# Expert gathers of two slots for 64 tokens, and their products in pairs on the two column halves of TensorE

## The chip, the cores and the metric

The kernel runs on one core of a Trainium2 chip. The metric is the device time of one execution in microseconds (us), the median of several runs. Engines are called as in the profile: PE (TensorE, matrix products; PEld its weight loads), DVE (VectorE), ACT (ScalarE), POOL (GpSimd, which here issues the gathers), SP (SyncE, which issues the weight loads), and 16 DMA engines.

## What is computed

A diffusion backbone of two layers on 256 context tokens and 256 latent tokens, D = 1024, all in float32. Each layer is a modulated norm, attention (two head groups), an output projection, and then an expert feed-forward (PEER). The second layer leaves out the context's outputs. The change is in the expert part, for which six blocks of 128 tokens are worked through (four in layer 0, two in layer 1):

```python
q = (xb @ p['peer_wq']).reshape(PEER_CHUNK, PEER_HEADS, 2, PEER_KEY_HALF)
s = jnp.einsum('thcd,ckd->thck', q, p['peer_subkeys'])
sv, si = lax.top_k(s, PEER_TOPK)
...
top_s, pos = lax.top_k(cand_s, PEER_TOPK)
eidx = ...                                   # 8 heads x 16 = 128 experts per token
gate = jax.nn.softmax(top_s, axis=-1)
u = jnp.take(p['peer_u'], eidx, axis=0)
v = jnp.take(p['peer_v'], eidx, axis=0)
act = jax.nn.gelu(jnp.einsum('ted,td->te', u, xb), approximate=False) * gate
return jnp.einsum('te,ted->td', act, v)
```

So each token takes 128 rows of 8 KB (u and v side by side) out of a table, and the whole kernel gathers 768 times 128 rows.

## The kernel before

**Slots.** A block has 128 slots. Slot i of a block is the i-th expert of each of its 128 tokens, one token per partition. POOL (unit, L613) copies eight slots' indices from IDX to FIX (L626) and issues one indirect DMA per slot (L634) into one of the eight buffers of the ring EXPERT; before it, it waits until the buffer's last user is done. DVE (dot, L1541) multiplies the u half of the buffer with H2, the block's normed tokens, and sums: one dot product per token. ACT (weigh, L1117) takes the GELU (L1122), multiplies with the gate (L1124), and for three slots of four scales the identity by the result to DIAG (L1129, three buffers). PE (apply, L932) multiplies DIAG with the v half into the two banks VSUM (L937), which sums the slots. Every fourth slot's product is DVE's instead (apply, L1548, line L1554), added to ACC after the next slot's dot product. After 128 slots `close` (L1576) adds both sums, multiplies with the modulation's gate, which PE broadcasts from a diagonal matrix GD (L813), and adds to the tokens X. The next block's first slots stand behind it on DVE, and its first product on PE waits until both banks are read.

**Picks.** For each head and tile, `top` (L1479) finds the 16 best experts on DVE, ACT's `gate_exps` (L1112) takes their exponentials with the sum (TE, TSUM), and `experts` (L1513) turns positions into expert indices: two small operations and a conversion (L1518), six wide ones on one-hot tables (L1174, L1527), the inverse of the sum (L1529), and then GATE (L1535) and IDX (L1537). DVE waits for ACT's sum just ahead of L1529. On ACT the exponential stands behind the weighing of the slots ahead of it and needs another table than GELU.

**Weights.** SP loads weights in pieces of up to 512 KB into the five buffers of WT (WSLOTS), each as soon as PE has released the piece five before it. Where the projections use them: L797, L825, and L927 for the picks' queries (two pieces per head).

**The order of the work.** A plan written out by code, one list of stages, is walked by all engines. `weave` (L189) spreads slots evenly through the background (picks, projections, attention of the next tiles) by a table of costs. ACT and DVE follow `late(PLAN)`, in which slots stand earlier by up to three (LEAD_SLOTS) than on PE. Stages of the plan: front (norm and input projections), attention (L850, L1062, L1366), outward (output projection, norm, and `back`, which turns the normed tokens for H2, L1247), pick. Gathers run from 244 us to the end, except while the modulation products of layer 1 (`ada`, L740: matmuls on four groups of 32 columns, L755) use the ring's buffers, 1840 to 1990 us. In time: picks at 244 to 345 us, attention to 410, output projection to 480, picks to 590, the latents' front to 775, attention to 915, output to 1025, picks to 1370, layer 1's front to 1835; after the modulation picks to 2125, front and attention to 2280, output to 2345, and picks to the end.

A float32 product is two instructions in the trace: a slot's two products of 128x512 are four MATMULs.

## Time and profile before

| | |
|---|---|
| median of 3 runs | 2744.06 us (2742.5 to 2751.88) |
| the profiled execution | 2754.68 us, its span 2752.7 us |
| PE busy | 2116.2 us, 77% of the span, clock 0.892 |
| DVE busy | 1852.3 us, 67% |
| ACT busy | 1146.0 us, 42% |
| POOL busy | 973.3 us, 35% |
| DMA | 976.17 MB, mean 355 GB/s; 855.69 MB of it by POOL's queue |
| chain that ended last | PE 31%, DVE 24%, DMA 23%, ACT 13% |

A profile is one execution. The busy share of an engine is a mean over stretches with different limits. The chain is followed back from the last instruction, at each step to what released it. The clock is the part of full speed that was granted to PE. A DMA share is that of the 16 engines' time; it can come out a little above 1.

### The profile page before, as it was taken

How to read it: one execution, taken by the hardware profiler on the slowest of the kernel's cores; microseconds unless marked ns; L12 is line 12 of the kernel's file. 1: busy time of each engine (PE TensorE's matmuls, PEld its weight loads, DVE VectorE, ACT ScalarE, POOL GpSimd, SP SyncE). 2: the span in 40 equal slices, each digit the busy share in tenths (PEclk: the TensorE clock that was granted, in tenths of full speed). 3: DMA queues.
4: the chain of work that ended last, by engine and by line, in shares of the span. 5: the costliest groups of instructions: out<-in, count | busy, mean ns of one | idle time of the engine just before them, and what ended most of it. 6: DMA issues, size and time to landing. Idle time of an engine off the chain costs nothing.

```text
span 2752.7 us, 26089 instructions
## 1 busy us (share of the span) xinstructions
PE 2116.2 (77%) x6768; PEld 1091.3 (40%) x6768; DVE 1852.3 (67%) x4482; ACT 1146.0 (42%) x3024; POOL 973.3 (35%) x916
## 2 busy tenths in 40 slices
PE   6997788779898987777677777768777887767765
PEld 2455434534444444343233332334544444433321
DVE  0145985975678769888956565543389696877775
ACT  2122483452388444344452342322135573433432
POOL 1012343333344333344443443420033443444443
PEclk8988889889999999889899999988788999888989
DMA  8467989989899899899998999994299999999997
GB/s 323 136 235 304 387 338 357 389 320 383 318 380 343 326 369 375 355 418 416 415 420 363 418 394 414 413 386 155 75 355 400 393 369 396 402 392 420 421 416 296
DMA packets 210712, 976.17 MB, mean 355 GB/s; under 512 B 17532, under 2 KB 70296, under 8 KB 112280
## 3 DMA queue, kind: packets, MB, share of 16 engines
q0 software_dynamic: 123648, 855.69, 77.2%
q1 hardware_dynamic: 86936, 118.99, 12.6%
q8 instruction: 54, 0.88, 0.1%
q14 instruction: 74, 0.61, 0.1%
HBM read 973.56 MB, written 1.05 MB: 354 GB/s over the span
## 4 chain that ended last, share of the span: by engine, by line
PE 31%; DVE 24%; DMA 23%; ACT 13%; issue 7%; POOL 1%; POOLq 0%; SPq 0%; DVEq 0%; ACTq 0%
DMA EXPERT<-in_peer_uv,FIX 21%; PE VS L937 11%; PE PA L797 9%; DVE EXPERT L1544 8%; DVE ACC L1554 3%; PE PA L825 2%; DVE SCR L1174 2%; ACT L1122 2%; PE PB L927 2%; DMA EXPERT<-in_w_ada 2%; ACT L1070 1%; ACT WEI L1124 1%; ACT HT L1026 1%; ACT DIAG L1129 1%; PE VS L755 1%
## 5 line engine op out<-in xcount | busy, mean ns | idle before, releaser
L937 PE MATMUL VS<-EXPERT,DIAG 128*128 128x512 f32 x2304 | 1185.8, 656 | 322.3 <-ACT DIAG L1129 322.1
L634 POOL DMA_INDIRECT EXPERT<-in_peer_uv,FIX x768 | 899.4, 1171 | 1169.7 <-PE VS L937 760.3
L1544 DVE CUSTOM_DVE_ANT_0 EXPERT<-EXPERT,H 128x1024 f32<-128x1024 f32 x768 | 925.5, 1223 | 363.3 <-DMA EXPERT<-in_peer_uv,FIX 354.4
L937 PEld LDWEIGHTS VS<-EXPERT,DIAG 128*128 128x128 f32 x2304 | 457.1, 209 | 920.2 <-issue 468.2
L1122 ACT ACTIVATE GEL<-DOT 128x1 f32<-128x1 f32 x768 | 155.3, 202 | 1060.3 <-DVE DOT L1544 1059.5
L797 PE MATMUL PA<-WT,HT 128*128 128x512 f32 (+2 forms) x768 | 328.0, 574 | 31.2 <-ACT KTD L1052 10.4
L1554 DVE SCALAR_TENSOR_TENSOR ACC<-EXPERT,WEI,ACC 128x1024 f32<-128x1024 f32 x192 | 246.0, 1281 | 40.6 <-ACT WEI L1124 39.9
L1129 ACT ACTIVATE DIAG<-IDN,WEI 128x128 f32<-128x128 f32 x576 | 231.3, 402 | 74.0 <-PE VS L937 56.0
L1124 ACT ACTIVATE WEI<-GEL,GATE 128x1 f32<-128x1 f32 x768 | 226.3, 295 | 25.0
L797 PEld LDWEIGHTS PA<-WT,HT 128*128 128x128 f32 x768 | 150.7, 199 | 193.8 <-issue 140.2
L927 PE MATMUL PB<-HT,WT 128*128 128x128 f32 (+1 forms) x1280 | 204.3, 320 | 10.4 <-issue 10.4
L927 PEld LDWEIGHTS PB<-HT,WT 128*128 128x128 f32 x1280 | 192.4, 216 | 36.6 <-issue 30.0
L626 POOL COPY FIX<-IDX 128x8 uint32 (+1 forms) x96 | 39.1, 408 | 316.1 <-PE VS L937 179.9
L1122 ACT ACT_TABLE_LOAD x115 | 147.5, 1283 | 6.6 <-ACT SCR L1070 0.8
L664 POOL DMA_DIRECT2D EXPERT<-in_w_ada x48 | 34.6, 722 | 262.3 <-PE VS L755 193.8
L726 PE MATMUL PB<-IDN,SCR 128*128 128x128 f32 (+1 forms) x374 | 58.8, 305 | 74.7 <-ACT SCR L1015 21.9
L726 PEld LDWEIGHTS PB<-IDN,SCR 128*128 128x128 f32 (+1 forms) x374 | 47.5, 152 | 107.4 <-ACT SCR L1015 28.0
L908 PE MATMUL PA<-SKT,SCR 128*128 128x128 f32 x192 | 37.9, 338 | 59.1 <-ACT SCR L1106 59.1
L1070 ACT ACTIVATE SCR<-PB,NM 128x512 f32<-128x512 f32 (+1 forms) x96 | 58.8, 614 | 52.7 <-DVE NM L1392 52.0
L825 PE MATMUL PA<-WT,HT 128*128 128x512 f32 (+1 forms) x136 | 67.2, 645 | 16.3 <-ACT HT L1058 8.7
L755 PE MATMUL VS<-EXPERT 128*32 128x512 f32 x384 | 55.5, 688 | 22.1 <-DMA EXPERT<-in_w_ada 22.1
L1375 DVE TENSOR_REDUCE MX<-PB 128x1 f32<-128x512 f32 (+1 forms) x96 | 55.4, 596 | 22.2 <-PE PB L865 22.0
(140 smaller groups left out, 1715.6 us busy)
## 6 DMA issues: line engine op xcount, KB each, us to landing
EXPERT<-in_w_ada POOLq DMA_DIRECT2D x48, 1024.0 KB, 10.2
WT<-in_peer_wq SPq DMA_DIRECT2D x80, 512.0 KB, 15.4
WT<-in_w_in SPq DMA_DIRECT2D x56, 512.0 KB, 10.9
WT<-in_w_out SPq DMA_DIRECT2D x40, 512.0 KB, 7.7
EXPERT<-in_peer_uv,FIX POOLq DMA_INDIRECT x768, 11.6
WT<-in_w_in SPq DMA_DIRECT2D x16, 384.0 KB, 9.7
WT<-in_w_in SPq DMA_DIRECT2D x20, 288.0 KB, 6.9
WT<-in_mla_wk_up SPq DMA_DIRECT2D x5, 512.0 KB, 10.2
```

The costliest lines, as they stand in the source:

```text
L634: pool.indirect_dma_start(out=EXPERT[:, j, :], out_offset=None, in_=a["peer_uv"], in_offset=bass.IndirectOffsetOnAxis(ap=FIX[:, par, j:j + ...
L726: last = nc.tensor.transpose(bank[0:rows, i * P:(i + 1) * P], s, IDN[:, :])
L797: last = nc.tensor.matmul(bank[:, 0:n], HT[:, k, t * P:(t + 1) * P], w[:, k % KP, 0:n], start=(k == 0), stop=(k == KD - 1))
L825: last = nc.tensor.matmul(bank[:, 0:n], HT[:, k0 + k, t * P:(t + 1) * P], w[:, k % KP, 0:n], start=(k == 0), stop=(k == kn - 1))
L927: last = nc.tensor.matmul(bank[:, mine], held["w"][k // HP][:, k % HP, c * P:(c + 1) * P], HT[:, k, mine], start=(k == 0), stop=(k == KD - 1))
L937: ins = nc.tensor.matmul(VSUM[n][:, :], DIAG[:, i, :], EXPERT[:, j, D + n * W:D + (n + 1) * W], start=first, stop=last_one)
L1070: ins = nc.scalar.activation(PR[:, h % 2, c, 0:keys], bank[:, 0:keys], ACT.Exp, bias=NM[:, h % 2, c:c + 1], scale=SC_M if h < MH else SC_D ...
L1122: nc.scalar.activation(GEL[:, one], DOT[:, j:j + 1], ACT.Gelu).then_inc(gelu_ready, 1)
L1124: nc.scalar.activation(WEI[:, one], GEL[:, one], ACT.Copy, scale=gate).then_inc(wei_ready, 1)
L1129: nc.scalar.activation(DIAG[:, i, :], IDN[:, :], ACT.Copy, scale=WEI[:, one]).then_inc(diag_ready, 1)
L1544: nc.vector.tensor_tensor_reduce(out=EXPERT[:, j, 0:D], in0=EXPERT[:, j, 0:D], in1=H2[:, b % HB, :], scale=1.0, scalar=0.0, op0=ALU.mult, ...
L1554: nc.vector.scalar_tensor_tensor(out=ACC[:, :], in0=EXPERT[:, j, D:2 * D], scalar=WEI[:, BY_PE:BY_PE + 1], in1=ACC[:, :], op0=ALU.mult, op ...
```

## The change

A gather now brings two slots for 64 tokens. Partitions 0 to 63 hold the even slot and 64 to 127 the odd slot of the same 64 tokens; of two gathers that follow each other the first (g = 0) is for tokens 0 to 63, the second for 64 to 127. Sizes and number of the gathers stay. For this IDX and GATE are written in four pieces each (64 partitions, every second column), GATE by ACT, which waits for DVE's inverse, now taken right behind the conversion L1518. H2 holds each half of the tokens twice (four copies in place of one) and has two blocks instead of three, so the last `back` of layer 0 moves behind the picks. DIAG is 128x64, one for each of the ring's eight buffers, scaled from TWO, two stacked identities. PE takes two gathers at a time, with matmuls that write partitions 0 to 63 and 64 to 127 of VSUM in turn. All products are PE's; ACC shrinks to 512 columns and serves `close` alone. WT has four buffers instead of five, and LEAD_SLOTS is four.

```diff
-WSLOTS = 5
+WSLOTS = 4
...
-HB = 3
+HB = 2
+IB = 3
+G = P // 2
...
-LEAD_SLOTS = 3
+LEAD_SLOTS = 4
...
-            def apply(no, i, j, first=False, last_one=False):
-                pe.wait_ge(diag_ready, no + 1)
+            def apply(no, j, first=False, last_one=False):
+                pe.wait_ge(diag_ready, no + 2)
                 for n in range(2):
-                    ins = nc.tensor.matmul(VSUM[n][:, :], DIAG[:, i, :], EXPERT[:, j, D + n * W:D + (n + 1) * W],
-                                           start=first, stop=last_one)
-                ins.then_inc(used_pe, 1)
+                    for g in range(2):
+                        ins = nc.tensor.matmul(VSUM[n][g * G:(g + 1) * G, :], DIAG[:, j + g, :],
+                                               EXPERT[:, j + g, D + n * W:D + (n + 1) * W], start=first, stop=last_one)
+                        if n == 1:
+                            ins.then_inc(used_pe, 1)
...
+                act.wait_ge(inverse_ready, tick("inverse"))
+                for g2 in range(2):
+                    mine = slice(g2 * G, (g2 + 1) * G)
+                    parted = TE[mine, t, :].rearrange("p (q s) -> p q s", s=2)
+                    for s in range(2):
+                        to = GATE[s * G:(s + 1) * G, b % IB, h * TOPK:(h + 1) * TOPK].rearrange("p (q g) -> p q g", g=2)
+                        ins = nc.scalar.activation(to[:, :, g2], parted[:, :, s], ACT.Copy, scale=TINV[mine, t:t + 1])
+                link(ins)
...
-                if i < BY_PE:
-                    act.wait_ge(wei_ready, no + 1)
-                    if not isinstance(mine, int) or mine >= BY_PE:
-                        act.wait_ge(used_pe, mine - BY_PE + 1)
-                    nc.scalar.activation(DIAG[:, i, :], IDN[:, :], ACT.Copy, scale=WEI[:, one]).then_inc(diag_ready, 1)
+                act.wait_ge(wei_ready, no + 1)
+                nc.scalar.activation(DIAG[:, j, :], TWO[:, :], ACT.Copy, scale=WEI[:, one]).then_inc(diag_ready, 1)
...
-                    nc.vector.tensor_copy(H2[:, b % HB, half * W:(half + 1) * W], bank[:, :]).then_inc(emptied_a, 1)
+                    for g2 in range(2):
+                        for s in range(2):
+                            ins = nc.vector.tensor_copy(H2[s * G:(s + 1) * G, b % HB, g2, half * W:(half + 1) * W],
+                                                        bank[g2 * G:(g2 + 1) * G, :])
+                    ins.then_inc(emptied_a, 1)
...
                 after(mark(nc.vector.tensor_copy(ABF[:, :, :], AB[:, :, :])))
+                dve.wait_ge(topexp_ready, tick("topexp"))
+                nc.vector.reciprocal(TINV[:, t:t + 1], TSUM[:, t:t + 1]).then_inc(inverse_ready, 1)
...
-                dve.wait_ge(topexp_ready, tick("topexp"))
-                inverted = mark(nc.vector.reciprocal(TINV[:, t:t + 1], TSUM[:, t:t + 1]))
                 after(found)
-                at = slice(h * TOPK, (h + 1) * TOPK)
...
-                after(inverted)
-                nc.vector.tensor_scalar(GATE[:, b % HB, at], TE[:, t, :], TINV[:, t:t + 1], None, ALU.mult)
                 after(both)
-                nc.vector.tensor_scalar(IDX[:, b % HB, at], PICK[:, 0, :], float(l * NK * NK), None, ALU.add)\
-                    .then_inc(idx_ready[t], 1)
+                for g2 in range(2):
+                    parted = PICK[g2 * G:(g2 + 1) * G, 0, :].rearrange("p (q s) -> p q s", s=2)
+                    for s in range(2):
+                        to = IDX[s * G:(s + 1) * G, b % IB, h * TOPK:(h + 1) * TOPK].rearrange("p (q g) -> p q g", g=2)
+                        ins = nc.vector.tensor_scalar(to[:, :, g2], parted[:, :, s], float(l * NK * NK), None, ALU.add)
+                ins.then_inc(idx_ready[t], 1)
...
                 diagonals(l, tile // 2, 2, 0)
-                dve.wait_ge(used_dve, (b + 1) * QUADS)
-                dve.wait_ge(used_pe, (b + 1) * QUADS * BY_PE)
                 for n in range(2):
                     half = slice(n * W, (n + 1) * W)
-                    if n == 1:
-                        diagonals(l, tile // 2, 2, n)
-                    tt(ACC[:, half], ACC[:, half], VSUM[n][:, :], ALU.add).then_inc(vsum_read, 1)
                     rows = from_a()
+                    link(nc.vector.tensor_copy(ACC[:, :], rows[:, :]))
+                    free_a()
+                    if n == 0:
+                        diagonals(l, tile // 2, 2, 1)
+                        dve.wait_ge(used_pe, (b + 1) * SLOTS)
+                    tt(ACC[:, :], VSUM[n][:, :], ACC[:, :], ALU.mult).then_inc(vsum_read, 1)
                     dve.wait_ge(vsum_read, 2 * b + n + 1)
-                    link(tt(ACC[:, half], ACC[:, half], rows[:, :], ALU.mult))
-                    free_a()
                     x = X[:, tile, half]
-                    ins = tt(x, x, ACC[:, half], ALU.add)
+                    ins = tt(x, x, ACC[:, :], ALU.add)
```

## Rows read from the trace of the kernel before

**Rows 1.** Table by stretch: stretch, us, busy PE, PEld, DVE, ACT, POOL; clock, DMA share, GB/s.
```profile
345.00:410.00 65.00, 52.41 (x165) 25.71 (x164) 52.39 (x131) 57.34 (x117) 26.57 (x22) 0.89 0.89 334
410.00:480.00 70.00, 57.12 (x189) 30.94 (x188) 42.03 (x88) 28.11 (x77) 23.50 (x24) 0.93 0.95 357
480.00:590.00 110.00, 79.62 (x333) 52.63 (x331) 104.61 (x365) 54.85 (x133) 38.85 (x36) 0.86 0.98 381
590.00:700.00 110.00, 99.89 (x244) 45.75 (x244) 54.36 (x88) 35.25 (x109) 34.55 (x33) 0.95 0.92 352
700.00:775.00 75.00, 61.31 (x196) 33.97 (x197) 53.37 (x101) 31.23 (x90) 25.24 (x24) 0.91 0.82 327
775.00:915.00 140.00, 122.21 (x470) 65.42 (x469) 117.75 (x245) 121.36 (x230) 54.41 (x48) 0.98 0.89 339
915.00:1025.00 110.00, 96.82 (x295) 50.97 (x294) 72.32 (x129) 47.91 (x134) 42.20 (x40) 0.95 0.95 363
1025.00:1110.00 85.00, 66.99 (x188) 36.18 (x187) 83.33 (x281) 41.05 (x104) 32.17 (x32) 0.90 0.97 380
1110.00:1835.00 725.00, 533.00 (x1254) 242.26 (x1253) 497.97 (x1055) 274.69 (x822) 308.89 (x287) 0.88 0.99 402
...
2040.00:2125.00 85.00, 61.09 (x228) 37.44 (x226) 80.18 (x271) 42.18 (x110) 32.40 (x32) 0.86 1.02 412
2125.00:2345.00 220.00, 179.35 (x580) 93.33 (x581) 156.62 (x298) 122.32 (x299) 84.92 (x77) 0.92 0.96 383
2345.00:2740.00 395.00, 272.02 (x713) 120.69 (x711) 290.94 (x639) 147.62 (x455) 184.35 (x164) 0.89 0.98 403
```

**Rows 2.** Chain of waits by line, 605 to 700 us and 775 to 915 us.
```profile
by line: PE PA L797 55.4%; PE VS L937 36.1%; DVE SCR L1174 2.2%; DVE SCR L1298 1.2%; ACT QTD L1052 1.1%; ACT KTD L1052 1.1%; PE PB L726 0.9%; issue 0.9%; DVE SCR L1307 0.5%; ACT HT L1026 0.4%; DVEq L1317 0.1%; DVE SS L1307 0.1%; DVEq L1170 
...
by line: ACT L1122 12.8%; ACT L1070 11.9%; DVE EXPERT L1544 11.4%; ACT SCR L1070 8.3%; issue 7.0%; DVE ACC L1554 5.3%; PE VS L937 5.2%; DVE MX L1375 5.2%; PE PB L865 4.6%; DVE SCR L1389 4.4%; ACT WEI L1124 3.7%; PE PA L873 3.5%; ACT GEL L11
```

**Rows 3.** Expert product in the chain; PE around the modulation product: start, us, line, count.
```profile
647.36 1.72 PE VS L937 x4
...
1994.03 3.74 PE L927 MATMUL PB<-HT,WT 128*128 128x128 f32 x32
1997.70 3.64 PE L755 MATMUL VS<-EXPERT 128*32 128x512 f32 x32
```

**Rows 4.** Groups by form: line, engine, operation, count; busy us, mean ns; idle before.
```profile
L1554 DVE SCALAR_TENSOR_TENSOR ACC<-EXPERT,WEI,ACC 128x1024 f32<-128x1024 f32 x192 | 246.0, 1281 | 40.6 <-ACT WEI L1124 39.9 <-DVE SCR L1293 0.3 <-DVE EXPERT L1210 0.2
...
L1129 ACT ACTIVATE DIAG<-IDN,WEI 128x128 f32<-128x128 f32 x576 | 231.3, 402 | 74.0 <-PE VS L937 56.0
L1124 ACT ACTIVATE WEI<-GEL,GATE 128x1 f32<-128x1 f32 x768 | 226.3, 295 | 25.0
```

**Rows 5.** One pick in order of time, DVE and ACT: start, us, engine, line.
```profile
2072.08 0.18 DVE L1518 CAST ABF<-AB 128x32 f32<-128x32 uint32 x1
...
2073.97 0.19 ACT L1114 ACTIVATION_READ_ACCUMULATOR TE<-TS,NT 128x1 f32 x1
...
2074.30 0.15 DVE L1529 RECIPROCAL TINV<-TSUM 128x1 f32<-128x1 f32 x1
...
2075.00 1.23 DVE L1544 CUSTOM_DVE_ANT_0 EXPERT<-EXPERT,H 128x1024 f32<-128x1024 f32 x1
```

**Rows 6.** Closing block 0 on DVE, in order of time, to the next block's first slot.
```profile
700.68 1.28 DVE L1554 SCALAR_TENSOR_TENSOR ACC<-EXPERT,WEI,ACC 128x1024 f32<-128x1024 f32 x1
...
708.12 0.69 DVE L1174 TENSOR_TENSOR ACC<-ACC,PA 128x512 f32<-128x512 f32 x1 [1.57 <-PE PA L813]
...
710.88 1.22 DVE L1544 CUSTOM_DVE_ANT_0 EXPERT<-EXPERT,H 128x1024 f32<-128x1024 f32 x1
```

**Rows 7.** Group by form: the copies to H2.
```profile
L1252 DVE COPY H<-PA 128x512 f32<-128x512 f32 x12 | 7.9, 687 | 19.8 <-PE PA L726 19.7
```

**Rows 8.** A weight piece in the chain, and PE's wait for it in order of time.
```profile
2142.66 16.42 DMA WT<-in_w_in
...
2159.12 1.56 PE L797 MATMUL PA<-WT,HT 128*128 128x384 f32 x4 [1.75 <-DMA WT<-in_w_in]
```

92 lines of the change are left out of this document (38 added, 54 removed).

## The prediction

> **What bounds the kernel now.** I read three views in order. First the table by stretch [rows 1], which splits the time in which experts are gathered. The reader should compare, line by line, the share of the DMA engines with the busy times of DVE, PE and ACT: where the DMA share is close to 1 the gathers themselves set the pace, and nothing that an engine saves there is worth anything. That holds for 1110 to 1835 us and 2345 to 2740 us, 1120 us together (0.99 and 0.98 with the closes in them). In the rest the share is 0.82 to 0.98, and an order of work that is interleaved with the gathers sets the pace. Second, the chain of waits of two such stretches [rows 2]: 605 to 700 us is PE alone (input projection 55.4%, expert products 36.1%); 775 to 915 us is attention, where ACT leads (two table loads per head and slot, L1070 and L1122, 24.7%) and DVE's share of the expert product (L1554) has 5.3%. Third, the picks (480 to 590, 1025 to 1110, 2040 to 2125 us in [rows 1]): DVE is busy 104.61 of 110, 83.33 of 85 and 80.18 of 85 us. There DVE sets the pace, with DMA close behind (0.97 to 1.02).
>
> If every stretch of [rows 1] with a share below 1.01 came up to it (its length times the part that it lacks), 345 to 410 gives 7.7 us, 410 to 480 4.2, 480 to 590 3.3, 590 to 700 9.8, 700 to 775 14.1, 775 to 915 16.6, 915 to 1025 6.5, 1025 to 1110 3.4, 1110 to 1835 14.4, 2125 to 2345 10.9 and 2345 to 2740 11.7: about 103 us. That is the ceiling of any gain here.
>
> **The products on PE.** A slot's product is now four matmul instructions of 128x512 in 1.72 us at full clock [rows 3], for three slots in four: 1.29 us per slot on average. Afterwards two slots are eight instructions on 64 columns each. If the two column halves run side by side they take about 1.72 us for two slots, 0.86 us per slot; if not, 3.44 us, 1.72 per slot. The nearest row is the modulation product L755 on four column groups of 32: 32 instructions in 3.64 us, 0.11 us each [rows 3], a quarter of the 0.43 us of a full-width one. So column groups do overlap in this kernel with the same operand shapes, and I take 0.86, a saving of 0.43 us per slot, and keep 1.72 as the other end. A switch of form seems free: L755 starts at 1997.70 us, 0.07 us before the modelled end of the work ahead of it (1994.03 + 3.74) [rows 3]. The Trainium skill, page "TensorEngine Tiling (Array Packing)", section "Key Properties", speaks against this: changing the tiling mode drains the engine. It has no price; here there would be two switches per pair, 768 in all, and the row shows none that can be read.
>
> Where PE leads and DMA has room are 410 to 480, 590 to 700 and 915 to 1025 us, by the plan some 17 + 30 + 30 slots. The saving is 77 x 0.43 / 0.94 (clock) = 35 us on PE, but DMA room there is 4.2 + 9.8 + 6.5 = 20.5 us, and some of the time in them is spent waiting for norms and gates, not PE. I take 12 us (ends 4 and 20).
>
> **DVE without its quarter.** 192 products of 1.281 us [rows 4] leave DVE, 1.20 us each from start to start. In attention (345 to 410, 775 to 915, about half of 2125 to 2345) they stand on the chain with about 5% [rows 2], as does PE's product (5.2%), while ACT is busy 57 of 65 and 121 of 140 us and gets more: DIAG for four slots in four instead of three, at half the width. At 0.402 us for 128 columns and 0.295 us for one [rows 4] 64 columns come to about 0.35 us: 4 x 0.35 against 3 x 0.40 is +0.05 us per slot, 5 us for the 96 slots. Out of 320 us, 5% is 16 us for the DVE share and 5 us for PE's third, minus 5 for ACT, with room on DMA of 7.7 + 16.6 + 5: I take 13 us saved (ends 3 and 25).
>
> **The handshake in each pick.** This speaks against the change. Before, DVE reads ACT's exp sum only after its six wide operations on the one-hot tables; GATE is then DVE's. Afterwards DVE waits for the sum right behind the conversion L1518, inverts it for ACT, and does the wide operations after that. In [rows 5] the conversion ends at 2072.26, ACT's sum at 2074.16 us. ACT can't be earlier: it has just weighed the slot whose dot product DVE did before the pick, and then loads a table. That gap was covered by DVE's own 2.04 us (2072.26 to 2074.30); now it is bare. The same rows can be read for 48 picks, and 43 have such a gap, of 1.1 to 2.3 us; where it is short of 2.3 the last slot had no DIAG, which it now gets (0.35 us). Behind the inverse come 2.04 us of wide operations, 0.1 and four small IDX writes of 0.1 each where one stood. From 2072.26 to the next dot product at 2075.00 is 2.74 us now; afterwards 1.90 + 0.35 + 0.15 + 2.04 + 0.1 + 0.5 = 5.0. That is +2.3 here, between +1.6 and +2.4 in the others, 2.1 on average. Queued behind the wait on DVE are the next dot products, so ACT, PE and POOL wait for it too. ACT's four GATE pieces (under 0.3 us each by WEI [rows 4]) lie beside the wide operations and cost nothing; without that cover 1.2 us per pick.
> In the picks that DVE paces (25, between 275 and 345, 480 and 590, 1025 and 1110, 2040 and 2125 us) that is +53 us, against 26 DVE products less, 26 x 1.20 = 31 us: **+21 us** (ends +8, if ring and DMA took part of it, and +30). In the others (1110 to 1370, 2345 to 2740) DMA leads and DVE has the time: 4.7 slots or more save 1.4 and the pick costs 2.1, while DVE is busy 69 and 74% of those two stretches [rows 1]: nothing.
>
> **Closing a block.** A close takes DVE from 700.68 to 710.88 us [rows 6], 10.2 us with the ring full and POOL idle. It loses the product (1.2) and the memset ahead of the first slot, and the second gate diagonal is made before the first half is finished, so that PE's second broadcast no longer waits for it (1.57 us of idle DVE [rows 6]): 7 to 8 us are left. Against that the first pair of the next block needs two dot products before PE starts. For blocks 0 to 3 I take 2.3 us each, 9 us. For blocks 4 and 5, closed right behind their last slot, PE's last pair (1.7 us after ACT's DIAG) is now on the way to the broadcast, and eats the gain: 0.
>
> **Copies for H2.** One copy of 0.687 us [rows 7] becomes four on 64 partitions, of the same free size: 8 instead of 2 per block, +3.7 us on DVE, six times. DVE is idle a third of the time or more around them (410 to 480, 915 to 1025 us, the prologue) and one is put behind the picks: 2 us in all, 22 if nothing hid them.
>
> **Four weight buffers for five.** Pieces of w_in take up to 16.42 us on the chain [rows 8], and PE already waited 1.75 us with five buffers. Issue to use shrinks by one piece. At 12 pieces between 2133 and 2175 us, each limited to latency over buffers, 16.4/4 - 16.4/5 = 0.8 us, 10 us; elsewhere pieces are further apart (3.4 us and more) or come sooner. The output projection at 2280 adds a little. I take 8 us (ends 0 and 18). Moving slots one further ahead of the background in late() (LEAD_SLOTS 4) is to pay for the pair's delay; I count both as 0 (ends -5 and +5), since a slot that waits for the next product was already there, one in four.
>
> **Sum.** -12 - 13 + 21 - 9 + 2 + 8 = **-3 us** against the span of 2752.7 us (2754.68 us for that execution), so about 2750 us there. The profiled execution lies 10.6 us above the median of the runs, 2744.06; the same sum from the median gives **2741 us**.
>
> **Rivals.**
> A, relief to the DMA limit: with two engines relieved at once, everything outside the picks comes up close to DMA's pace. Of the ceiling of 103 us, 96 lie outside the picks; two thirds of it, 62 us, less 21 for the picks and 8 for weights is -33: 2711 us. For it: in 775 to 915 us all three engines are busy 84 to 87%, so chains between them, not one engine, hold it up. Against it: ACT's table loads stay.
> B, slower: the bare wait for the exp sum. It decides as soon as it exceeds what a cycle of picks loses, 1.2 us per pick with four slots. With the long end for the picks (+30), the weights at +15, and relief of only 25 us in all: +20, 2764 us. For it: DVE at 94 to 98% in those stretches [rows 1].
> C, the change doesn't do what it says: the halves don't overlap, 0.43 us more per slot instead of less. 77 slots cost 35 us instead of gaining 12, attention about 10 more: some 60 us above, 2800 us. Against it stands L755 [rows 3].
> D, the clock: granted 0.98 in 775 to 915 us, where PE is busy 87%, and 0.86 to 0.90 in the picks with 72 to 79% [rows 1]. With PE at 75% in attention it may fall to that level, and take 10% of PE's work back, about 5 us; it is inside the range of the forecast. The Trainium skill, "TensorE: Matmul & The Clock Gate", section "What's actually happening", says that activity releases a throttle, of two levels; by that rule this loss comes too, and the trace agrees in its direction.
>
> **How the numbers follow.** Forecast with its spread (2727 to 2757) 0.42, A 0.30, B 0.21, C 0.07. A change of under 0.3%, 8 us (2736 to 2752), is what a measurement of this kernel can't tell from none. Of the forecast's own case about a quarter lies below, over half inside, a fifth above. Faster: 0.30 + 0.10 = 0.40. Slower: 0.21 + 0.07 + 0.08 = 0.36. Same: 0.24. The range from 2700 to 2777 leaves out C and the far ends of A and B; the forecast's own is 2727 to 2757.
>
> **What the changed profile would show.** The product line on PE: 128x64 instructions, eight in about 1.9 us, and PE's busy time down (overlap counted once); 3.4 us per pair would prove C. DVE's reciprocal L1529 with 80 to 90 us idle before it, released by ACT's TE, against 5 now: if it is under 30, the pick step is wrong and the kernel faster by up to 20 us. Pick cycles 1 us longer. Attention and projections with a DMA share up by some hundredths: if not, relief was worth nothing. PE waits for WT in 2130 to 2170 us longer than 1.75 us. The DMA-paced stretches with the same time per gather: if they are slower, holding two slots at a time drained the ring, which I count at nothing.

## The result, and the profile after

The change makes the kernel slower: 2850.48 us, median of the runs (2848.94 to 2861.48), against 2743.72 us (2742.5 to 2751.88) for the kernel before on the same chip. The ratio is 1.0386, with a 95% interval from 1.0359 to 1.0413: 106 us. The forecast was 2741 us with a range from 2700 to 2777. The profiled execution took 2851.5 us, its span is 2849.7 us.

Head of the profile of the kernel after:

```profile
span 2849.7 us, 27355 instructions
...
PE 1941.4 (68%) x7536; PEld 878.7 (31%) x7536; DVE 1670.7 (59%) x4417; ACT 1241.4 (44%) x3408; POOL 926.7 (33%) x916
...
PE 30%; DMA 25%; DVE 21%; ACT 16%; issue 6%; POOL 2%; POOLq 0%; SPq 0%; DVEq 0%; ACTq 0%; PEld 0%
```

PE has 175 us less to do than before (2116.2) and DVE 182 us less (1852.3); ACT has 95 us more (1146.0 before), at 44% of the span. The kernel takes 97 us more by the two spans. So the loss isn't work of PE or DVE; those two wait. The table by stretch says where. The columns are those of [rows 1]; the stretches are cut so that they hold about the same slots as lines there (by DVE's dot products to within 4, for example 38 against 41 in attention and 27 against 31 in the picks of 480 to 590 us):

```profile
359.00:431.00 72.00, 49.76 (x188) 21.15 (x188) 47.71 (x126) 61.66 (x132) 24.42 (x24) 0.80 0.80 298
431.00:500.00 69.00, 52.98 (x218) 25.44 (x220) 38.92 (x84) 25.80 (x77) 20.36 (x22) 0.85 0.95 365
500.00:615.00 115.00, 70.18 (x338) 44.14 (x334) 93.35 (x364) 58.07 (x157) 34.15 (x33) 0.81 0.89 343
...
812.00:945.00 133.00, 111.97 (x478) 54.65 (x478) 97.84 (x215) 115.12 (x225) 45.77 (x43) 0.86 0.79 307
945.00:1060.00 115.00, 90.70 (x319) 43.25 (x316) 64.86 (x124) 50.46 (x146) 42.80 (x40) 0.88 0.92 357
1060.00:1155.00 95.00, 63.67 (x230) 28.03 (x228) 78.04 (x284) 48.03 (x134) 36.29 (x34) 0.79 0.90 354
1155.00:1875.00 720.00, 445.96 (x1474) 160.59 (x1473) 423.98 (x1006) 292.78 (x910) 293.12 (x281) 0.82 0.96 391
2078.00:2184.00 106.00, 64.44 (x288) 36.31 (x284) 83.14 (x304) 51.08 (x146) 35.49 (x34) 0.76 0.93 365
2184.00:2420.00 236.00, 173.86 (x675) 76.08 (x671) 140.54 (x288) 129.69 (x323) 85.83 (x83) 0.86 0.92 364
```

Read the DMA share (the last but one number) against [rows 1]. It was to rise wherever engines held it down; it rose nowhere, stayed at 0.95 in the output projection (410 to 480) and fell in the other eight lines: picks of 480 to 590 us from 0.98 to 0.89 and of 1025 to 1110 from 0.97 to 0.90, attention of 775 to 915 from 0.89 to 0.79, and even the DMA-paced 1110 to 1835 from 0.99 to 0.96. In the picks DVE is now busy 93.35 of 115 us, no longer 104.61 of 110: it doesn't set the pace by its work any more, it waits.

The delay can also be counted by slots, as the start of the same slot's dot product on DVE in the two traces. By the times of before it is 11.2 us at 345, 13.0 at 480, 28.8 at 590, still 28.7 at 915, 36.0 at 1025, 46.9 at slot 256 (1118 us), 52.7 at slot 512 (2014 us), 81.0 at 2345 and 95.2 at the last slot. So the picks of 480 to 590 us lose 16 us and those of 1025 to 1110 lose 11, the stretch from 2014 to 2345 us 28, attention at 775 to 915 nothing, and the two DMA-paced stretches 6 and 14.

The groups of the change, by form (as [rows 4]): busy time, mean ns, idle time just before:

```profile
L936 PE MATMUL VS<-EXPERT,DIAG 128*64 128x512 f32 x3072 | 917.2, 733 | 464.3 <-ACT DIAG L1137 456.1
L1137 ACT ACTIVATE DIAG<-TWO,WEI 128x64 f32<-128x64 f32 x768 | 267.0, 348 | 25.0
L1125 ACT ACTIVATE GATE<-TE,TINV 64x8 f32<-64x8 f32 x192 | 57.5, 300 | 18.8 <-DVE TINV L1532 15.7 <-issue 1.3
L1550 DVE TENSOR_SCALAR IDX<-PICK 64x8 uint32<-64x8 f32 x192 | 33.5, 174 | 3.5
L1262 DVE COPY H<-PA 64x512 f32<-64x512 f32 x48 | 33.1, 689 | 22.5 <-PE PA L724 21.8
...
L1532 DVE RECIPROCAL TINV<-TSUM 128x1 f32<-128x1 f32 x48 | 7.9, 164 | 100.9 <-ACT TE L1117 93.5 <-issue 7.1
```

The durations are as forecast: DIAG 348 ns (0.35 was taken), the H2 copy 689 ns as [rows 7], an IDX piece 174 ns (0.1 was taken). The inverse has 100.9 us of idle time before it, 2.1 per pick, 93.5 of it put down to ACT's exp sum. And the two waits that grew, from the list of waits (total us, times, longest), of before and then of after:

```profile
POOL EXPERT L634 <- PE VS L937: 760.3, 300, 15.4
DVE EXPERT L1544 <- DMA EXPERT<-in_peer_uv,FIX: 354.4, 270, 4.5
POOL EXPERT L634 <- DVE ACC L1554: 194.6, 76, 7.6
POOL FIX L626 <- PE VS L937: 179.9, 60, 15.6
```

```profile
POOL EXPERT L634 <- PE VS L936: 928.1, 214, 17.6
DVE EXPERT L1557 <- DMA EXPERT<-in_peer_uv,FIX: 550.6, 362, 7.7
...
POOL FIX L629 <- PE VS L936: 323.0, 75, 21.5
```

POOL waits for a free buffer 116 us longer (928.1 + 323.0 against 760.3 + 194.6 + 179.9), and DVE waits 196 us longer for a gather to land. PE has less to do and releases buffers later. That is the shape of the loss: the ring is held by something that isn't PE's or DVE's work.

Do the halves overlap at all? One pair in the output of the timeline, in order of time:

```profile
660.20 1.94 PE L936 MATMUL VS<-EXPERT,DIAG 128*64 128x512 f32 x8
...
662.07 2.41 PE L795 MATMUL PA<-WT,HT 128*128 128x512 f32 x5
```

Eight instructions in 1.87 us from start to start, where one full-width slot took 1.72 us for four [rows 3], both with the full clock granted. They do.

### The profile page after: what moved, and what is told of

Its sections match the earlier page's. It is cut to its first block, busy times and chain, and to the rows that moved or that the text cites. A ratio compares the mean times of both kernels' runs of the same rounds, so it can differ in the third digit from the quotient of the medians.

```text
span 2849.7 us, 27355 instructions
## 1 busy us (share of the span) xinstructions
PE 1941.4 (68%) x7536; PEld 878.7 (31%) x7536; DVE 1670.7 (59%) x4417; ACT 1241.4 (44%) x3408; POOL 926.7 (33%) x916
## 4 chain that ended last, share of the span: by engine, by line
PE 30%; DMA 25%; DVE 21%; ACT 16%; issue 6%; POOL 2%; POOLq 0%; SPq 0%; DVEq 0%; ACTq 0%; PEld 0%
DMA EXPERT<-in_peer_uv,FIX 23%; PE VS L936 11%; PE PA L795 9%; DVE EXPERT L1557 8%; DVE SCR L1181 3%; ACT L1133 2%; PE PA L823 2%; ACT WEI L1135 2%; ACT L1071 2%; ACT DIAG L1137 2%; ACT L1117 2%; ACT HT L1027 1%; POOL EXPERT L634 1%; PE PB L925 1%; DMA EXPERT<-in_w_ada 1%
## 5 line engine op out<-in xcount | busy, mean ns | idle before, releaser
L634 POOL DMA_INDIRECT EXPERT<-in_peer_uv,FIX x768 | 860.5, 1120 | 1173.4 <-PE VS L936 928.1
L936 PE MATMUL VS<-EXPERT,DIAG 128*64 128x512 f32 x3072 | 917.2, 733 | 464.3 <-ACT DIAG L1137 456.1
L936 PEld LDWEIGHTS VS<-EXPERT,DIAG 128*64 128x64 f32 x3072 | 226.2, 162 | 1024.0 <-ACT DIAG L1137 606.1
L795 PE MATMUL PA<-WT,HT 128*128 128x512 f32 (+2 forms) x768 | 347.0, 601 | 44.5 <-ACT KTD L1053 20.3
L1137 ACT ACTIVATE DIAG<-TWO,WEI 128x64 f32<-128x64 f32 x768 | 267.0, 348 | 25.0
L925 PE MATMUL PB<-HT,WT 128*128 128x128 f32 (+1 forms) x1280 | 219.0, 335 | 25.6 <-issue 20.8
L925 PEld LDWEIGHTS PB<-HT,WT 128*128 128x128 f32 x1280 | 199.5, 226 | 64.0 <-issue 49.1
L629 POOL COPY FIX<-IDX 128x8 uint32 (+1 forms) x96 | 31.4, 327 | 451.9 <-PE VS L936 323.0
L724 PEld LDWEIGHTS PB<-IDN,SCR 128*128 128x128 f32 (+1 forms) x374 | 50.2, 162 | 148.7 <-ACT SCR L1016 46.9
L823 PE MATMUL PA<-WT,HT 128*128 128x512 f32 (+1 forms) x136 | 67.7, 649 | 22.4 <-ACT QTM L1048 11.2
L906 PEld LDWEIGHTS PA<-SKT,SCR 128*128 128x128 f32 x192 | 33.3, 251 | 141.3 <-ACT SCR L1107 126.9
```

What stands on the lines that cost most here:

```text
L634: pool.indirect_dma_start(out=EXPERT[:, j, :], out_offset=None, in_=a["peer_uv"], in_offset=bass.IndirectOffsetOnAxis(ap=FIX[:, par, j:j + ...
L724: last = nc.tensor.transpose(bank[0:rows, i * P:(i + 1) * P], s, IDN[:, :])
L795: last = nc.tensor.matmul(bank[:, 0:n], HT[:, k, t * P:(t + 1) * P], w[:, k % KP, 0:n], start=(k == 0), stop=(k == KD - 1))
L823: last = nc.tensor.matmul(bank[:, 0:n], HT[:, k0 + k, t * P:(t + 1) * P], w[:, k % KP, 0:n], start=(k == 0), stop=(k == kn - 1))
L925: last = nc.tensor.matmul(bank[:, mine], held["w"][k // HP][:, k % HP, c * P:(c + 1) * P], HT[:, k, mine], start=(k == 0), stop=(k == KD - 1))
L936: ins = nc.tensor.matmul(VSUM[n][g * G:(g + 1) * G, :], DIAG[:, j + g, :], EXPERT[:, j + g, D + n * W:D + (n + 1) * W], start=first, stop= ...
```

## The experiments

All runs come with their own runs of the kernel before (median 2745.1 to 2747.2 us by batch). Differences below are made from the ratios, times 2745 us. By the intervals of the two ratios a difference between two runs is uncertain by some 10 to 15 us to either side, and by 6 to 9 where both have ten executions. Line names are those of the kernel that is edited.

### The three parts of the change, each undone

**Inverse late, GATE on DVE.** In the changed kernel, the order of before in a pick, with GATE in four pieces on DVE:

```diff
-                dve.wait_ge(topexp_ready, tick("topexp"))
-                nc.vector.reciprocal(TINV[:, t:t + 1], TSUM[:, t:t + 1]).then_inc(inverse_ready, 1)
...
+                dve.wait_ge(topexp_ready, tick("topexp"))
+                inverted = mark(nc.vector.reciprocal(TINV[:, t:t + 1], TSUM[:, t:t + 1]))
```

> The kernel after, but DVE takes the inverse after the wide operations again and writes GATE itself in four pieces; ACT no longer waits for the inverse. Theory handshake (the bare wait for the exp sum on DVE makes most of the loss): idle of DVE ahead of the reciprocal falls from 101 us to under 10, and the time from 2850 to 2800 us or less. Theory pair (a slot that waits for its partner keeps its buffer, the ring of eight runs dry): 2835 us or more, since the ring is not touched. Theory weights (four buffers): no more than 10 us.

Measured: 2818.88 us (2817.03 to 2821.65), ratio 1.0262 [1.0233, 1.0291]. 34 us of the 106 come back, between the two numbers (2800 for the wait as most of the loss, 2835 for the pair). DVE's idle time ahead of the inverse falls from 100.9 to 13.5 us. GATE moves from ACT to DVE in the same edit, so the 34 us are those of both.

**Single slots.** PE takes each slot as soon as its DIAG is ready; halves, ring and order stay:

```diff
-                pe.wait_ge(diag_ready, no + 2)
+                pe.wait_ge(diag_ready, no + 1)
+                g = j % 2
...
-                            for k in range(0, TOPK, 2):
+                            for k in range(TOPK):
```

> The kernel after, but PE takes each slot as soon as its DIAG is ready, two products on one column half, instead of waiting for two slots. A lone slot costs PE 1.72 us at full clock instead of 0.86. Theory pair: buffers come free earlier, 2850 falls to 2810 us or less in spite of PE's dearer products. Theory handshake: 2840 to 2860 us, as PE is not the bound of the picks. If PE time were the bound: slower than 2860 us.

Measured: 2817.61 us (2815.06 to 2821.0), ratio 1.0258 [1.0229, 1.0288]: 35 us, as much as the item before, and I had counted it at 0. The theory of the pair wanted 2810 us or less, that of the wait 2840 or more; it lies nearer to the first. PE's products take 1155.4 us instead of 917.2, that is 238 us more work on PE, and the kernel is faster. One place shows why, first in the kernel after (DVE's dot of the first slot of a pair, the dot of the second behind the pick, the product):

```profile
1385.68 1.23 DVE L1557 CUSTOM_DVE_ANT_0 EXPERT<-EXPERT,H 128x1024 f32<-128x1024 f32 x1 [1.78 <-DMA EXPERT<-in_peer_uv,FIX]
...
1389.67 0.16 DVE L1532 RECIPROCAL TINV<-TSUM 128x1 f32<-128x1 f32 x1 [2.38 <-ACT TE L1117]
...
1392.80 1.22 DVE L1557 CUSTOM_DVE_ANT_0 EXPERT<-EXPERT,H 128x1024 f32<-128x1024 f32 x1
...
1396.37 5.90 PE L936 MATMUL VS<-EXPERT,DIAG 128*64 128x512 f32 x14 [9.55 <-ACT DIAG L1137]
```

and the same slot with single products:

```profile
1383.00 1.23 DVE L1556 CUSTOM_DVE_ANT_0 EXPERT<-EXPERT,H 128x1024 f32<-128x1024 f32 x1 [1.26 <-DMA EXPERT<-in_peer_uv,FIX]
...
1385.23 1.93 PE L936 MATMUL VS<-EXPERT,DIAG 128*64 128x512 f32 x4 [0.56 <-ACT DIAG L1136]
```

From dot to product it is 10.7 us in the first and 2.2 in the second. The order by single slots puts the second half of a pick between the two slots of a pair; the first one's buffer is held through it. Counted over DVE's whole timeline, 20 of the 48 inverses stand behind an odd number of dots, that is inside a pair.

**Both undone.** 

> The kernel after with both edits tried alone: inverse and GATE late and on DVE, and each slot's product as soon as its DIAG is ready. If handshake and pair cost each their own (32 and 33 us alone) the two add up: 2785 us. If both show one and the same wait: 2815 us.

Measured: 2791.05 us (2789.31 to 2806.23), ratio 1.0173 [1.0138, 1.0209]: 58 us of 106. The parts nearly add up (69 by themselves), nearer to the 2785 us of two separate costs than to 2815.

**Five weight buffers in the changed kernel.** DIAG is laid into the used-up u half of the ring buffer, which makes room for the fifth:

```diff
-WSLOTS = 4
+WSLOTS = 5
-        DIAG = sb("DIAG", [P, RING, G])
+        DIAG = EXPERT[:, :, 0:G]
```

> The kernel after with five weight buffers. The room comes from DIAG, which lies in the spent u half of its ring buffer instead of a tile of its own; instructions and waits are the same. Theory weights, by the 45 us that four buffers cost the kernel before: 2850 falls to 2805 to 2815 us, first in the picks of block 0 and in the slots 27 to 50 of block 4. Theory handshake or pair alone: 2840 us or more, as the prefetch then hides behind other waits.

Measured: 2838.72 us (2834.51 to 2854.68), ratio 1.0341 [1.03, 1.0382]: 12 us, no more than the uncertainty of such a difference. With the two edits above as well:

> The changed kernel with late inverse and GATE on DVE, each slot's product as soon as its DIAG is ready, and five weight buffers instead of four. The same without the fifth buffer ran at 2791 us; the kernel before at 2744 to 2747 us. Theory 1 (the weight buffers cost the changed kernel as much as the kernel before, 42 us, once the pair and the early wait no longer hide it): 2750 to 2760 us, and the change is explained but for some 10 us. Theory 2 (in the changed kernel the fifth buffer is worth 12 us only, as it was with the pairs): 2779 us, and some 32 us stay for the copies to H2, the four pieces of IDX and GATE, the order with four slots ahead.

Measured: 2769.94 us (2764.96 to 2777.34), ratio 1.0088 [1.0058, 1.0119]. Here the fifth buffer is worth 23 us: neither of the two numbers, but nearer to the small one. With the 47 us below, the order is that it pays more the less else holds the kernel up; the step from 12 to 23 alone isn't clear of noise.

### The same parts, put into the kernel before

**The early wait alone.** The wait and L1529 of the kernel before moved behind L1518, nothing else:

> The kernel before, with nothing changed but the place of the wait for the exp sum and of the reciprocal on DVE: right behind the conversion, as in the kernel after. GATE stays on DVE. Theory handshake as forecast: 26 picks that DVE paces lose about 2 us each, 2744 to 2795 us; by the long end 85 us. Theory pair or weights: the wait is taken up by the ring, under 2760 us.

Measured: 2802.35 us (2789.76 to 2805.3), ratio 1.0184 [1.0144, 1.0225]: 51 us, between 40 and 62 by the interval. The gross price of the forecast was 53. DVE's idle time before the inverse goes from 5.2 to 89.6 us.

**Four weight buffers alone** (`WSLOTS = 4`):

> The kernel before with four weight buffers instead of five, nothing else. Forecast was 8 us, ends 0 and 18: 2744 to 2752 us. Theory weights (the smaller prefetch makes most of the loss): 2790 us or more.

Measured: 2788.64 us (2784.11 to 2806.67), ratio 1.0171 [1.0121, 1.0221]: 47 us, where the forecast had 8. The groups that changed are those of the picks' queries, the kernel before first, then the run with one place of its timeline:

```profile
L927 PE MATMUL PB<-HT,WT 128*128 128x128 f32 (+1 forms) x1280 | 204.3, 320 | 10.4 <-issue 10.4
L1106 ACT COPY SCR<-PB 128x128 f32<-128x128 f32 (+1 forms) x80 | 21.9, 273 | 67.3 <-PE PB L927 67.1
```

```profile
L927 PE MATMUL PB<-HT,WT 128*128 128x128 f32 (+1 forms) x1280 | 201.2, 317 | 58.3 <-issue 58.3
L1106 ACT COPY SCR<-PB 128x128 f32<-128x128 f32 (+1 forms) x80 | 22.0, 275 | 118.2 <-PE PB L927 118.2
...
503.80 3.75 PE L927 MATMUL PB<-HT,WT 128*128 128x128 f32 x16 [9.02 <-issue]
507.59 0.27 ACT L1106 COPY SCR<-PB 128x128 f32<-128x128 f32 x1 [10.59 <-PE PB L927]
...
510.12 0.94 POOL L634 DMA_INDIRECT EXPERT<-in_peer_uv,FIX  x1 [18.55 <-PE VS L937]
```

PE's idle time before the query product goes from 10.4 to 58.3 us, and only the number of weight buffers differs. The trace files it under "issue"; that it is the landing of these pieces is concluded from the edit, as the trace doesn't name them. Each head wants two pieces of 512 KB, and a piece takes 15.4 us to land (median of the page's DMA issues of before), while a piece is issued only when the one four before it is released. While PE stands there, ACT stands behind it in L1106 with the weighing of the next slots queued behind (the 10.59 us above), and POOL behind these (18.55 us without a free buffer).

**Six weight buffers.** In the kernel before, with H2 in two blocks to make room:

> The kernel before with six weight buffers instead of five, paid for by H2 with two blocks instead of three, for which the last turn of the latents' tokens goes behind the picks, as in the change. Theory 1 (weight loads between gathers are limited by their latency over the number of buffers, and five is short too): part of the 42 us that the fifth buffer brought comes again, 2715 to 2735 us, faster than the kernel before. Theory 2 (five covers the latency, and the step from four to five is where it ended): 2740 to 2750 us, or some us more for the moved turn.

Measured: 2745.66 us (2738.3 to 2759.28), ratio 1.0007 [0.9984, 1.0029]. No gain, as the second theory had it: five is deep enough here, and the moved `back`, which is part of this edit, costs nothing that shows.

**All products on PE.** The kernel before with the fourth slot's product on PE too, at full width, by single slots:

> The kernel before with DVE's quarter of the products on PE at full width, one slot at a time: no pairs, no new layout, five weight buffers, the late wait. DVE loses 192 x 1.2 us, PE gains 192 x 1.72 us. By the forecast's terms the picks gain 31 us, the closes 6, attention 10, the stretches that PE paces lose 20: 2715 to 2730 us. If relief of DVE is worth nothing: 2745 us or more.

Measured: 2757.96 us (2748.25 to 2765.63), ratio 1.0033 [1.0016, 1.0051]: 9 us slower. By slot it is 8.4 us ahead at slot 97 of block 0 (its dot starts at 578.6 us against 587.0), behind the picks, and loses that and more in the front and the attention that follow (7.9 us behind at slot 200). Taking the products off DVE and putting them on PE brings nothing.

**The same with DIAG in the ring**, eight instead of four:

> Single slots at full width, all on PE, as in the run of 2758 us, with DIAG in the ring (eight). ACT waited 135 us for PE before a DIAG there. Theory 1 (these waits are slack that comes back as a later wait of PE): 2752 to 2762 us. Theory 2 (they held up the weighing and the exponentials of the picks behind them on ACT): 2735 to 2748 us, as fast as the kernel before or a little faster.

Measured: 2753.84 us (2744.39 to 2769.05), ratio 1.0044 [1.0017, 1.007]; not to be told from the run before it. At slot 97 it is 9.7 us ahead of the kernel before, 5.3 behind at slot 200.

### What the pair costs

**Pairs at full width.** The run above with four DIAG buffers, PE taking two slots at a time:

```diff
-                pe.wait_ge(diag_ready, no + 1)
+                pe.wait_ge(diag_ready, no + 2)
```

> The kernel before with all products on PE at full width, five weight buffers and the late wait, as in the run that came to 2758 us, but PE takes two slots at a time, as in the change, behind the second one's DIAG. Nothing of the halves, of the four-piece writes or of the copies. Theory 1 (holding the first slot of a pair is the cost, 33 us in the changed kernel): 2780 to 2800 us. Theory 2 (the 33 us belonged to the column halves, for example to the drain between forms or to the weights of 64 columns): no difference, 2755 to 2762 us.

Measured: 2850.38 us (2846.02 to 2852.67), ratio 1.0369 [1.0336, 1.0401]: 92 us more than with single slots, far outside both numbers. That run had a flaw: a pair of DIAGs held two of four buffers, and ACT waited 269.9 us for PE ahead of a DIAG, against 135.2. So with DIAG in the ring:

> Products in pairs at full width, all on PE, as in the run of 2850 us, but DIAG is written into the ring buffer's used-up u half, so there are eight and ACT never waits for PE before a DIAG. Theory 1 (most of the 92 us that pairing cost at full width was the lack of DIAG buffers, and holding a slot costs about what it costs in the changed kernel): 2785 to 2800 us. Theory 2 (a pair of full-width products, 3.4 us on PE in one piece, is itself the cost, and the halves are what makes pairs bearable): 2830 us or more.

Measured: 2824.12 us (2819.34 to 2835.88), ratio 1.0286 [1.0241, 1.033]: 66 us more than single slots with the same DIAGs. That lies between the two numbers: lack of DIAG explains 23 us of the 92 (8 to 38 by the intervals), the pair itself the rest. At full width the second slot costs PE another 1.72 us in one piece. On the halves a pair costs 35 us, 24 with the inverse late (2818.88 against 2791.05), although single slots take that gain in PE's time away; the halves don't turn the pair into a gain. How much of the step from 66 to 35 is due to them isn't shown, as the two kernels differ in more.

**Slots placed in pairs.** The plan and `late` put slots two at a time, so no pick comes between them:

```diff
-    return [("slots", b, i, i + 1) for i in range(first, last)] + ([("close", b)] if last == SLOTS else [])
+    return [("slots", b, i, i + 2) for i in range(first, last, 2)] + ([("close", b)] if last == SLOTS else [])
```

> The changed kernel with the order by single slots replaced by one by pairs: the plan and the earlier order of ACT and DVE hold slots two at a time, so both slots of a pair stand next to each other on every engine. Everything else stays. The changed kernel stands at 2850 us. Theory 1 (what the pair costs is that its first slot is held in the ring until the second, which the interleaved order puts a background step later): placing them side by side gives most of the 33 us back that taking single slots gave, so 2815 to 2830 us. Theory 2 (what the pair costs is the release of two ring buffers at a time and a product that starts two dot products late, wherever the slots stand): 2845 us or more, and up to 2870 us, since the background steps between slots then come in larger lumps.

Measured: 2835.83 us (2829.74 to 2838.68), ratio 1.0312 [1.028, 1.0345]: 20 us back, between the theories. With late inverse and five weight buffers:

> The changed kernel with late inverse and GATE on DVE, five weight buffers, and the order by pairs; products stay in pairs on the two column halves. If the order by pairs undoes the hold of the first slot, it comes to the time of the same kernel with single slots, 2750 to 2780 us. If the pair itself costs, some 30 us more, 2790 to 2810 us.

Measured: 2792.52 us (2785.88 to 2794.96), ratio 1.0156 [1.0123, 1.019]: 19 us above the same kernel with single slots in the order by slots (2769.94), as the second theory had it. With the lead of four slots a pair costs even side by side.

### The lead of the slots

**Three ahead instead of four**, with late inverse, single slots, five buffers (`LEAD_SLOTS = 3`):

> The changed kernel with late inverse, single slots and five weight buffers (2770 us), with slots three ahead on ACT and DVE instead of four. Theory 1 (the order with four ahead puts dots in front of work that is due, and holds the rest of the gap to the kernel before): 2755 to 2762 us. Theory 2 (the rest is the four-piece copies and index writes and the products that PE takes over): 2767 to 2777 us.

Measured: 2760.48 us (2752.2 to 2771.48), ratio 1.0054 [1.0033, 1.0075]: 9 us. **One pair ahead instead of two**, with the order by pairs (`LEAD_SLOTS = 2`):

> Pairs on the two halves, order by pairs, late inverse, five weight buffers (2792 us), with one pair of slots ahead on ACT and DVE in place of two. Theory 1 (the lead is too long, as with single slots, where three in place of four gave 9 us): 2775 to 2785 us. Theory 2 (a pair needs the lead, since PE waits for its second slot): 2795 us or more. To beat the kernel before it would have to come under 2740 us, which neither expects.

Measured: 2751.21 us (2747.19 to 2757.36), ratio 1.0021 [1.0008, 1.0034]: 37 us from one number in the order, more than either theory had. The two traces part most between slots 384 and 512, by 29 of 35 us, and one place in layer 1's front shows how. First with four ahead (PE's transpose, then the products behind it, POOL, and ACT's copy, for which PE waits):

```profile
1626.71 1.53 ACT L1048 COPY KTM<-PB 96x512 f32<-96x512 f32 x3
...
1627.33 1.09 PE L724 MATMUL PB<-IDN,SCR 128*96 128x128 f32 x4 [13.36 <-ACT KTM L1048]
1628.35 9.32 PE L936 MATMUL VS<-EXPERT 128*64 128x512 f32 x32
...
1632.83 0.94 POOL L634 DMA_INDIRECT EXPERT<-in_peer_uv,FIX  x1 [16.11 <-PE VS L936]
```

and with two ahead, for the same transpose:

```profile
1607.96 1.53 ACT L1048 COPY KTM<-PB 96x512 f32<-96x512 f32 x3
...
1608.58 1.09 PE L724 MATMUL PB<-IDN,SCR 128*96 128x128 f32 x4 [6.26 <-ACT KTM L1048]
...
1614.09 0.94 POOL L634 DMA_INDIRECT EXPERT<-in_peer_uv,FIX  x1 [9.91 <-PE VS L936]
```

Each slot that is placed ahead of this copy on ACT brings a wait for its gather, one per 2.49 us here. Six such weighings stand ahead of it in the first trace from 1612.70 us on, PE can't go on to the products of these very slots before its transpose, and all eight buffers are held until it does: POOL issues nothing for 16 us.

**And single slots on top:**

> The same with PE taking each slot as soon as its DIAG is ready. With the order by single slots and three ahead this kernel ran at 2760 us. Theory 1 (what the pair costs, even side by side, is that two ring buffers come free late and together): 10 to 20 us under the run beside it. Theory 2 (placed side by side, a pair costs nothing more and only the halves' overlap counts): the same as the run beside it or up to 10 us above it.

Measured: 2741.88 us (2733.05 to 2746.39), ratio 0.998 [0.9962, 0.9997]: 11 us under the run with pairs. It is the only variant of the change whose time isn't above that of the kernel before. It is ahead by 5 us, less than the 0.3% that a measurement of this kernel can tell from nothing.

### The clock

The granted clock went from 0.892 to 0.825 with the change. Behind each pair two products of full width with zero weights were added, which change nothing in the sum, to keep PE busy:

```diff
+                if not last_one:
+                    for n in range(2):
+                        nc.tensor.matmul(VSUM[n][:, :], ZERO[:, :], SKT[:, :, :].rearrange("p i n -> p (i n)"),
+                                         start=False, stop=False)
```

> The kernel after with two further full-width products of 128x512 behind each pair, with zeros as weights, so that PE has as much to do as with single slots (1.72 us per slot) but frees no buffer earlier. Theory clock (the kernel after is slow because an idler PE is granted less clock, 0.825 against 0.892): the clock rises to 0.88 and the time falls towards 2820 us, as with single slots. Theory pair: the clock rises, the time stays at 2850 us or gets longer by PE's extra work, up to 2900 us.

Measured: 2914.81 us (2910.07 to 2927.43), ratio 1.0611 [1.0573, 1.0649]. The time lies above both theories (2820 and up to 2900 us). The clock rose to 0.922 and the products' own time fell from 917.2 to 808.7 us; the 763.9 us of filler cost more. The lower clock isn't shown to be free, since the filler has a price of its own. But two kernels with about the same clock stand far apart (0.835 at 2751 us with pairs and two ahead, 0.832 at 2793 us with four ahead), and the first of them is within 6 us of the kernel before with its 0.892, so the clock doesn't explain the 106 us.

## Why the prediction was wrong, step by step

The whole difference can be walked in single edits, in us from the ratios. From after: single slots 35, late inverse and GATE on DVE 23 (34 when undone first), the fifth weight buffer 23 (12 when first), three slots ahead instead of four 9 (give or take 10). That leaves 15 (ratio 1.0054). All products on PE with DIAG in the ring, and nothing else of the change, stand at 12. What stays for the copies to H2, the four-piece IDX, the 64-column halves and the closes together is 3 us, with intervals of 6 to 7 us on either side of each of the two. Another order of the edits shares the 106 us out otherwise, as the two numbers in brackets show.

Set against the sum of the forecast, two steps failed. The relief terms (31 for DVE's products in the picks, 13 in attention, 12 for PE, 9 for the closes, less 2 for the copies: 63 us of gain) came out as the 15 us of loss that are left at the end of the walk, 78 us off. The pair and the lead, counted at 0, cost 44. The weight buffers add 15 us to what was taken (23 against 8), and the wait, taken at 53, cost 23 in the walk, 30 less. Together that is 107 us, the way from the forecast's -3 to the walk's 105 but for rounding.

- **The pair and the lead: 0 in the forecast (-5 to +5), 35 and 9 measured.** This is the step whose mechanism failed: a hold of the ring was put at nothing. I wrote that a slot that waits for the next product was already there, one in four. But it was DVE's, and DVE's own next dot was what it waited for. Now each pair's first slot waits for a dot that the order may place behind a pick or a background step, and in a ring of eight this is one gather less in flight. The last sentence of the prediction named the sign to look for (the DMA-paced stretch slower at the same work) and it is there, but small: a DMA share of 0.96 against 0.99, and 6 and 14 us in the two DMA-paced stretches, early waits included, of the 95 us in all. It should have been a rival with a price: 20 of 48 picks lie inside a pair, and the one shown above held a buffer 8.5 us longer, while gathers come one per 2.5 us.
- **Lead as a cure for the pair: wrong in sign.** A slot further ahead on ACT and DVE is ahead of work that PE needs before it can release anything, as the place in layer 1's front shows. 37 us in the order by pairs.
- **Four weight buffers: 8 in the forecast (0 to 18), 12 here, 23 and 47 elsewhere.** Mis-sized for the kernel before, and by a reading error: I looked at PE's waits for WT [rows 8], all of 1.75 us, and took the input projection as the only place. The picks' queries take two pieces per head, and their waits have no name in the trace. Latency over buffers was applied to the wrong consumer: the pieces for L927 take 15.4 us to land in the median, 80 times over, those of 512 KB for L797 10.9 us in the median, and the 16.42 us of [rows 8] is one of the long ones. By the same estimate 80 pieces at 15.4/4 - 15.4/5 = 0.77 us are 62 us, against 47 measured.
- **The wait in the picks: +53 gross in the forecast, 51 measured in the kernel before, 23 to 34 in the change.** The mechanism was right, and for the kernel before the size too; in the change, where the edit moves GATE as well, less comes back, as if part of it lay beside the other holds of the ring. The idle time before the inverse is 100.9 us, 2.1 per pick (80 to 90 in all was expected). The 31 us that I set against it, for the products that leave DVE in the picks, came by half at best: all products on PE brought 8.4 us through the picks of block 0 (some half of the 25 picks that DVE paces; counted by their inverses in the four windows they are 26) and lost them behind. Rival B was this wait, and gave 2764 us; it kept 25 us of relief and the weights at 15, and lacked the pair.
- **DVE and PE relieved: -12 on PE, -13 in attention and -31 in the picks in the forecast, no gain measured.** This is the largest error of the sum. DVE without its quarter and PE with all of it costs 9 to 12 us instead of gaining; PE has 284 us more of products (1469.9 against 1185.8), and the time is lost in the front and attention, where it was to pace. Less work on PE doesn't help either: at the end of the walk the halves by single slots have 308 us less of products on PE than all products at full width (1164.8 against 1473.0; DVE has 83 us more) and stand at 15 against 12. In pairs they come to 917.2 us, and nobody can use it: in the last two runs the kernel with 172 us more of products on PE (1094.1 against 922.0) is the faster by 11. Rival A, the relief to the DMA limit, didn't come in any run. The last run's trace is 20.3 us ahead of before at slot 224 and 11.0 at the last slot, but that trace of before took some 10 us more than its median, so this shows no gain clear of noise. Why no stretch used the relief isn't traced beyond these places.
- **Rival C fell.** Column halves overlap: 1.87 us for two slots. What the forecast said of the switch can now be bounded: 0.15 us per pair over the 1.72 of a full-width slot, two switches included. The Trainium skill, page "TensorEngine Tiling (Array Packing)", section "Key Properties", says that a change of tiling mode drains the engine; by this trace that costs 0.15 us or less per pair, 58 us of PE time at the very most over 384 pairs, on an engine that idles 464 us before these products.
- **The closes: -9 in the forecast.** From the dot of slot 120 of block 0 to that of slot 0 of block 1 it is 41.0 us instead of 51.3, and 1.1 us less for each of blocks 2 and 3 (2.3 were taken for each); block 1's, mixed with a pick, is 8.8 us longer, and block 4's 5.4 longer, where 0 was taken. But the same stretch takes 50.0 us when PE takes single slots, so most of the 10 us isn't the close's own work. It wasn't run by itself.
- **H2 copies: +2 forecast.** 33.1 us on DVE against 7.9, 25 us more where 22 were worked out, and with everything else some 3 us: not separated further.
- **Clock (rival D).** It fell as foreseen, to 0.86 in attention from 0.98. Its price wasn't measured; counted by slots, that stretch lost no time.

What stays open: whether the last run's 5 us are the halves' or the order's. It was 20 us faster than its twin with single-slot order and three ahead (1.0054), and PE's products took 1094.1 instead of 1164.8 us there, as two slots that are ready together overlap; the order by pairs at full width wasn't run.

## What to carry to other kernels

Joining two items of a ring into one operation can halve that operation, and makes the first item wait for the second; before counting the relief, find in the plan what may stand between the two, and price the ring slot held through it. A prefetch depth can be estimated as latency over depth at each consumer (62 us by it here, 47 measured), and a wait that the trace doesn't name ("issue") is to be compared with that before it is called slack. And when the engines already alternate in holding a ring up, taking busy time off two of them can leave the end where it was: the wait lists of the ring's producer and consumer say more than busy shares.

## What the runs showed of the hardware

- Two products on the two column halves, of 64 columns each, run side by side: eight instructions in 1.87 us against four of full width in 1.72, a factor of 1.84 for the pair. The Trainium skill, page "TensorE: Matmul & The Clock Gate", section "Measured speedup vs the span model", has 2.38 for three column tiles; this is the value for two here.
- DVE gains little from half the partitions and half the columns: an IDX write of 64x8 takes 174 ns, the whole one of 128x16 took 186; a GATE piece of 64x8 takes 242 ns (in the run with GATE on DVE), the whole one of 128x16 took 257. Four pieces cost nearly what four whole operations cost. On ACT a GATE piece takes 300 ns, and DIAG of 64 columns 348 ns against 402 for 128.
- A piece of weights of 512 KB for the picks' queries takes 15.4 us (median) to land beside the gathers, and the kernel before needs five buffers: four cost it 47 us, six bring nothing.
